# A bias table written two heads at a time in another stage, and Gram products of a recurrence taken in pairs

## The chip, the cores and the metric

One Trainium2 chip; the program uses one of its cores. The number compared is the device time of one execution in microseconds (us). The kernel before takes 2935.22 us, the median of three executions (2934.0 to 2938.29).

## The reference

Two blocks follow one another on 1024 tokens of width 1024, all in float32. The first has two layers. Layer 0 mixes by trailing means over 2, 4, 8 and 16 tokens, then a feed-forward part. Layer 1 is an attention over a window of 128 tokens, whose logits get a bias that depends on head and distance only:

```python
bias = rel_bias[t5_bucket(jnp.maximum(d, 0))]        # d = query - key, 16 heads
logits = logits + bias ...; logits = where(valid, logits, -inf)
```

Then again a feed-forward part. The second block projects the tokens and has two branches; one is a recurrence with eight heads of 64, in which every token updates a 64 x 64 state:

```python
sa = einsum('bhij,bhj->bhi', S, a_t)                  # a = -kk, b = kk * iclr ("ab" in the kernel)
S = S * w_t + sa[..., None] * b_t + v_t[..., None] * k_t
y = einsum('bhij,bhj->bhi', S, r_t)
```

## The kernel before, in words

The program is a row of stages. Each stage has one instruction list for each engine, and the next stage's lists start only when all engines have ended theirs, SyncE's (SP's) included. TensorE runs each float32 product as two matmul records.

**Pooling stage** (`pool_stage`, line 199). Nine tiles (16 meta tokens, then eight of 128). SP's list (line 240) loads x tiles six ahead, and at each tile t loads tile t + 6 if there is one (tiles 6 to 8 at t = 0 to 2) and stores tile t (`keep`, line 245), after the tile is made. It ends with a wait until all stores have landed.

**Projection stage of the attention** (`layer1_mixer`, line 1473, through `project_features`, line 881). Ten chunks of weights, numbered m = 0 to 9: keys, values, then eight of queries. A chunk is loaded (512 KB) by SP, multiplied by a gain on VectorE (line 988), split in a high and a low part on ScalarE (line 949) and VectorE (line 992), and multiplied on TensorE in two column slices of 24 matmuls each (lines 1032 to 1034). Three raw buffers. Three guests add work at each m:
- `KeyValueGuest` duplicates the keys by two DMAs at m = 4 (lines 1310, 1311) and turns the values at m = 4 to 6: three transposes on TensorE (line 1333), one copy on VectorE (line 1339). The transposes of m wait for the copy of m - 1.
- `BiasGuest` (line 1180): at m = 1 one matmul (line 1220) makes the bias by distance, 16 heads on 16 partitions x 384, which VectorE copies (line 1225). At m = 3 SP writes it to DRAM 128 times a head, one DMA of 3 MB (line 1203). At m = 7 it is read back with a shifted row for each partition (line 1208).
- `AdaGuest` (line 1228): eight loads of 1.5 MB (line 1254), for k = m - 1, each after the sum of k - 2, and one sum on VectorE each (line 1278).

In SP's list the load of chunk m stands after the guests of m - 1. In VectorE's list the order at m is: split of m + 1, gain of m + 2, the values' copy, the sum of k = m - 1.

**Recurrence** (`recurrence_stage`, line 1890). Eight tiles of 128 tokens, two chunks of 64 in each. The loop over tiles has ten half steps h. At each h TensorE works for three tiles at once: the preparation of tile t + 1, the inversion of tile t (lines 2261, 2273, 2275) and the chain through the state of tile t - 1. All products are of 64 x 64 by 64 columns, placed on one of four quarters of the array. Products of keys and reads are "Gram" products (line 2202): `inner` at h = 3 (24: ab with kk, eight of them twice, in the two orders of rows that are needed), `keys` at h = 6 (16: k with kk) and, in the chain, `rbk` at h = 4 (32: ab with r and k with r), 72 in a tile. VectorE masks them from the buffer `work_ps` (lines 2113, 2115, 2120, 2149). The tensors r and kk are planes 0 to 3 and 12 to 15 of one buffer, PB. At the start SP loads the masks, the bonus and the gates (1.5 MB) that only the stage after needs (line 2500).

Of the kernel before, what the change touches and what calls it, by code (L numbers as in the profile page):

```python
# [10 lines left out]
P = 128  # L11
# [187 lines left out]
def pool_stage(b, residual, store, post_gain, pre_gain):  # L199
# [6 lines left out]
    with b.stage() as ctx:  # L206
# [21 lines left out]
            "ss1", "sd1", "r1", "xg", "x", "ss2", "sd2", "r2", "xn", "tp", "xh", "xl", "stored")}  # L228

# [6 lines left out]
        with nc.Block() as block:  # L236
            @block.sync
            def _(sp):
# [22 lines left out]
                load(5)  # L261
                for t in range(N):
                    if t + XS < N:
                        load(t + XS)
                    keep(t)
                sp.wait_ge(s["stored"], 16 * N)

            @block.gpsimd
            def _(pool):
                pool.memset(b.eps[:, :], EPS).then_inc(s["eps"], 1)  # L270
                pool.wait_ge(s["bands"], 16)
# [49 lines left out]
            def _(dve):  # L321
# [6 lines left out]
                for k in range(N + 5):  # L328
# [34 lines left out]
                    if k + 2 < N:  # L363
                        inverted(k + 2)

            @block.tensor
            def _(pe):
# [7 lines left out]
                for k in range(N + 4):  # L375
                    if k < N:
# [15 lines left out]
                        if k == 0:  # L392
                            warm(3)
                    t = k - 4
                    if 0 <= t < N:
                        r = rows(t)
                        if t == 0:
                            pe.wait_ge(s["gains"], 48)
                        pe.wait_ge(s["xn"], t + 1)
# [780 lines left out]
class BiasGuest(Guest):  # L1180

    W = 3 * P

    def __init__(self, b, ctx, bias_rows, sinks):
        self.b, self.bias_rows, self.sinks = b, bias_rows, sinks
        self.table = b.nc.dram_tensor("bias_table", [HEADS, P, self.W], f32, kind="Internal").ap()
        self.rel = b.sb(ctx, "rel", [33, HEADS])
        self.hot = b.sb(ctx, "hot", [33, self.W])
        self.g = b.sb(ctx, "bias_by_offset", [HEADS, self.W])
        self.pb = b.ps(ctx, "pb", [HEADS, 512])  # L1190
        self.s_in, self.s_neg, self.s_g, self.s_ge, self.s_out, self.s_read = (
            b.sem(ctx, n) for n in ("bias_in", "bias_neg", "bias_g", "bias_ge", "bias_out", "bias_read"))

    def sync(self, sp, m):
        ins, table = self.b.ins, self.table
        if m == 0:
            sp.dma_start(self.rel[0:32, :], ins["rel_bias"]).then_inc(self.s_in, 16)
            sp.dma_start(self.hot[:, :], ins["cst"][0:33, C_HOT:C_HOT + self.W]).then_inc(self.s_in, 16)
            sp.dma_start(self.sinks[:, :], rows_of(ins["sinks"][0])).then_inc(self.s_in, 16)
# [4 lines left out]
        if m == 7:  # L1204
            sp.wait_ge(self.s_out, 16)

            skew = bass.AP(tensor=table.tensor, offset=P - 1, ap=[[self.W - 1, P], [P * self.W, HEADS], [1, 2 * P]])
            sp.dma_start(self.bias_rows[:, :, :], skew).then_inc(self.s_read, 16)
        if m > 7 and m == self.end:
            sp.wait_ge(self.s_read, 16)  # L1210
# [5 lines left out]
    def tensor(self, pe, m):  # L1216
        if m == 1:
            pe.wait_ge(self.s_in, 48)
            pe.wait_ge(self.s_neg, 1)
            pe.matmul(self.pb[:, 0:self.W], self.rel[:, :], self.hot[:, :], start=True, stop=True).then_inc(self.s_g, 1)  # L1220

    def vector(self, dve, m):
        if m == 1:
            dve.wait_ge(self.s_g, 1)
            dve.tensor_copy(self.g[:, :], self.pb[:, 0:self.W]).then_inc(self.s_ge, 1)
# [247 lines left out]
def layer1_mixer(b, residual_out, x1, ada_rows):  # L1473

    ins = b.ins
    with b.stage() as ctx:
# [6 lines left out]
        with b.stage() as c2:  # L1483
# [13 lines left out]
            bias = BiasGuest(b, c2, bias_rows, sinks)  # L1497
# [392 lines left out]
def recurrence_stage(b, PB, kk, ab, lw, tris, later):  # L1890
# [7 lines left out]
    with b.stage() as ctx:  # L1898
# [8 lines left out]
        RBK = b.sb(ctx, "RBK", [P, 2, DA])  # L1907
# [19 lines left out]
        pa = marks("pe_pre", ["cum", "ab", "ak", "tx", "tab", "tkv"])  # L1927
# [4 lines left out]
        pd = marks("pe_chain", ["ys0", "sa0", "st0", "rbk", "sa1", "ys1", "y0", "st1", "y1"])  # L1932
# [5 lines left out]
        da = marks("dve_pre", ["at", "bt", "kt", "lt", "xm", "rt", "ak"])  # L1938
        dl = marks("dve_add", [f"a{h}" for h in halves])
        dd = marks("dve_chain", ["sa00", "sa01", "sx0", "s0", "rb", "rk", "sa10", "sa11", "sx1", "s1"])  # L1940
# [34 lines left out]
        def natural():  # L1975
            quarters = wk[:, :, :].rearrange("p e (i x) -> p (e i) x", i=2)
            return quarters[:, 0:4:3].rearrange("p e (g x) -> p g e x", g=2)
# [7 lines left out]
        with nc.Block() as block:  # L1985
# [10 lines left out]
            def _(pool):  # L1996
# [3 lines left out]
                def other(t, l):  # L2000
                    da.wait(pool, t, "lt")
# [95 lines left out]
            def _(dve):  # L2097
# [12 lines left out]
                def masked(t):  # L2110
                    pa.wait(dve, t, "ab")
                    po.wait(dve, t - 2, f"u{LV - 1}")
                    da.mark(dve.tensor_tensor(LT[:, t % 2], natural(), wide(trix), ALU.mult), "lt")
                    pw.wait(dve, t - 2, "uu")
                    da.mark(dve.tensor_tensor(turned(t), wk[:, :, 0:4 * H].rearrange("p e (g x) -> p g e x", g=2), wide(lvl[0]), ALU.mult), "xm")

                def keys(t):
                    pa.wait(dve, t, "ak")
                    pm.wait(dve, t - 1, "mv")
                    da.mark(dve.tensor_tensor(halves_of(AK[:, :]), wk[:, :, 0:4 * H].rearrange("p e (g x) -> p e g x", g=2), wide(trix), ALU.mult), "ak")  # L2120
# [24 lines left out]
                def reads(t):  # L2145
                    pd.wait(dve, t, "rbk")
                    pd.wait(dve, t - 1, "y1")
                    for i, n in enumerate(("rb", "rk")):
                        dd.mark(dve.tensor_tensor(halves_of(RBK[:, i]), wk[:, :, 4 * H * i:4 * H * (i + 1)].rearrange("p e (g x) -> p e g x", g=2), wide(triu), ALU.mult), n)

# [3 lines left out]
                dve.wait_ge(s_in, 32)  # L2154
                masked(0)
                decayed(0, "rt")
                keys(0)
                for t in range(NT + 1):
                    more = t + 1 < NT
                    for h in halves:  # L2160
# [9 lines left out]
                        if h == 2 and more:  # L2170
                            decayed(t + 1, "kt")
                        if h == 3:
# [4 lines left out]
                        if h == 4 and t:  # L2177
                            stepped(t - 1, 0)
                            reads(t - 1)
                        if h == 5:  # L2180
                            if t:
                                applied(t - 1, 1)
                            if more:
                                decayed(t + 1, "rt")
# [6 lines left out]
            def _(pe):  # L2191
# [8 lines left out]
                def gram(left, right, t, e, c, q, place, part):  # L2200
                    o = 4 * H * part + H * c
                    return pe.matmul(wk[place, e, o:o + H], left[rows(e), c, chunk(t, q)], right[rows(e), c, chunk(t, q)], start=True, stop=True)

                def inner(t):
                    da.wait(pe, t, "bt")
# [4 lines left out]
                    for c in range(4):  # L2210
                        for q in range(2):
                            for e in range(2):
                                gram(ab, kk, t, e, c, q, at(e, q), 0)
                            mm = gram(ab, kk, t, 1, c, q, rows(q), 1)
                    pa.mark(mm, "ab")

                def keys(t):
                    da.wait(pe, t, "kt")
                    if t:
                        am.wait(pe, t - 1, "mv")  # L2220
                    else:
                        da.wait(pe, t, "xm")
                    for c in range(4):
                        for q in range(2):
                            for e in range(2):
                                mm = gram(k, kk, t, e, c, q, at(e, q), 0)
                    pa.mark(mm, "ak")

                def inverse_start(t):
                    pi.wait(pe, t, "eye")  # L2230
                    da.wait(pe, t, "ak")
# [46 lines left out]
                def values(t):  # L2278
                    da.wait(pe, t, "ak")
                    aa.wait(pe, t, "tkv")  # L2280
                    if t:
                        dd.wait(pe, t - 1, "rk")
                    else:
                        da.wait(pe, t + 1, "xm")
# [27 lines left out]
                def chain(t, n):  # L2312
# [27 lines left out]
                    elif n == "rbk":  # L2340
                        if t + 2 < NT:
                            da.wait(pe, t + 2, "xm")
                        else:
                            aw.wait(pe, t, "wt")
                        for c in range(4):
                            for i, left in enumerate((ab, k)):
                                for q in range(2):
                                    for e in range(2):
                                        mm = gram(left, r, t, e, c, q, at(e, q), i)
                    else:  # L2350
                        dd.wait(pe, t, "rk")
                        dd.wait(pe, t, "sx1" if q else "sa01")
                        for c in range(4):
                            for i, left in ((0, SA), (1, T[:, t % 3, 3])):
                                for e in range(2):
                                    mm = pe.matmul(yp[rows(e), P * c + H * q:P * c + H * (q + 1)], left[at(e, q), head(e, c)], RBK[at(e, q), i, head(e, c)],
# [4 lines left out]
                inner(0)  # L2361
                keys(0)
# [5 lines left out]
                steps = {1: ("ys0",), 3: ("sa0",), 4: ("st0", "rbk"), 5: ("sa1", "ys1"), 6: ("y0",), 7: ("st1",), 8: ("y1",)}  # L2368
                for t in range(NT + 1):
                    more = t + 1 < NT  # L2370
                    for h in halves:
# [7 lines left out]
                        if more:  # L2379
                            if h == 3:  # L2380
                                inner(t + 1)
# [312 lines left out]
```

## Time and profile before

| | |
|---|---|
| median of three executions | 2935.22 us |
| the profiled execution | 2935.99 us, of which span 2934.3 us |
| mean granted TensorE clock | 0.956 of full |
| pooling stage | 0 to 93 us |
| projection stage of the attention | 898 to 1061 us |
| recurrence | 2472 to 2748 us |

How to read it: the two long feed-forward stages (93 to 890 us and 1200 to 2000 us) keep TensorE busy nearly throughout; the change touches the other parts. PE is TensorE's matmul side, PEld its weight load, DVE VectorE, ACT ScalarE, POOL GpSimd, SPq SyncE's list. A wait row gives the engine and line that waited and what ended the wait; "issue" means that the profile shows nothing that it waited for. The share of DMA is of 16 engines.

### The profile page before, as it was taken

The page shows a single profiled execution, that of the slowest core. Times are in us where ns is not written, and L with a number is a line of the kernel's source. Part 1 is how long each engine was busy: PE and PEld are TensorE (multiplying, and loading weights), DVE is VectorE, ACT ScalarE, POOL GpSimd, SP SyncE. Part 2 cuts the span into 40 slices and gives each one's busy share as a digit, 9 for nine tenths or more (in the row PEclk, how much of TensorE's full clock was granted, in tenths as well). Part 3 has the DMA queues.
Part 4 walks back from the last instruction along what each step waited for, and adds up shares of the span by engine and source line. Part 5 has one row for each costly group of instructions (what it writes and reads, how often), then busy time and mean ns, then how long its engine had stood idle before and what let it go on. Part 6 is the DMA issues. An engine that isn't in the chain of part 4 may idle for free. (4 is left out here: it accounts for less than half of the span.)

```text
span 2934.3 us, 48957 instructions
## 1 busy us (share of the span) xinstructions
PE 2673.6 (91%) x20693; PEld 2221.3 (76%) x20693; DVE 1240.5 (42%) x2037; ACT 782.1 (27%) x1479; POOL 286.5 (10%) x190
## 2 busy tenths in 40 slices
PE   9799999999997699879999999999789998777776
PEld 8799999999986566667888888887577776766455
DVE  6333333333343458362333333333424553544447
ACT  6311111111153159342211111112221412233221
POOL 2100000000021025120000000002300000222102
PEclk9899999999998799989999999999899998999878
DMA  4211111111035500222111111112312112000032
GB/s 145 79 44 51 55 45 43 43 43 43 29 121 125 193 25 2 94 101 86 44 64 43 43 43 43 43 50 93 108 35 83 44 65 95 4 4 4 3 122 101
DMA packets 63099, 183.66 MB, mean 63 GB/s; under 512 B 10469, under 2 KB 19846, under 8 KB 61518
## 3 DMA queue, kind: packets, MB, share of 16 engines
q1 hardware_dynamic: 62928, 181.18, 18.6%
q8 instruction: 132, 2.16, 0.3%
q14 instruction: 39, 0.32, 0.0%
HBM read 150.54 MB, written 30.03 MB: 62 GB/s over the span
## 5 line engine op out<-in xcount | busy, mean ns | idle before, releaser
L790 PE MATMUL f0gu<-b1XH,f0w0H 128*128 128x346 f32 (+1 forms) x528 | 170.2, 322 | 6.9 <-DVE f0w0L L722 6.3
L742 DVE TENSOR_TENSOR f1hf<-f1sg,f1gu 128x512 f32<-128x512 f32 x44 | 30.3, 688 | 337.7 <-ACT f1sg L689 337.7
L742 DVE TENSOR_TENSOR f0hf<-f0sg,f0gu 128x346 f32<-128x346 f32 (+1 forms) x66 | 34.1, 516 | 326.2 <-ACT f0sg L689 326.2
L753 DVE TENSOR_TENSOR Y<-f0dn,Y 128x512 f32<-128x512 f32 (+1 forms) x180 | 124.0, 689 | 113.6 <-PE f0dn L837 112.7
L792 PE MATMUL f0gu<-b1XH,f0w0L 128*128 128x346 f32 (+1 forms) x528 | 170.3, 322 | 0.0
L791 PE MATMUL f0gu<-b1XL,f0w0H 128*128 128x346 f32 (+1 forms) x528 | 169.7, 321 | 0.0
L792 PE MATMUL f0gu<-b1XH,f0w1L 128*128 128x346 f32 (+1 forms) x528 | 169.7, 321 | 0.0
L790 PE MATMUL f0gu<-b1XH,f0w1H 128*128 128x346 f32 (+1 forms) x528 | 169.3, 321 | 0.0
L791 PE MATMUL f0gu<-b1XL,f0w1H 128*128 128x346 f32 (+1 forms) x528 | 169.0, 320 | 0.0
L753 DVE TENSOR_TENSOR Y<-f1dn,Y 128x512 f32<-128x512 f32 x160 | 109.2, 690 | 90.7 <-PE f1dn L837 90.7
L790 PE MATMUL f1gu<-b1XH,f1w0H 128*128 128x512 f32 x352 | 139.5, 396 | 6.3 <-DVE f1w0L L722 6.3
L835 PE MATMUL f0dn<-f0dH,f0hH 128*128 128x512 f32 (+1 forms) x360 | 142.5, 396 | 0.0
L836 PE MATMUL f0dn<-f0dL,f0hH 128*128 128x512 f32 (+1 forms) x360 | 142.3, 395 | 0.0
L837 PE MATMUL f0dn<-f0dH,f0hL 128*128 128x512 f32 (+1 forms) x360 | 140.9, 391 | 0.0
L791 PE MATMUL f1gu<-b1XL,f1w0H 128*128 128x512 f32 x352 | 140.0, 398 | 0.0
L792 PE MATMUL f1gu<-b1XH,f1w0L 128*128 128x512 f32 x352 | 139.3, 396 | 0.0
L791 PE MATMUL f1gu<-b1XL,f1w1H 128*128 128x512 f32 x352 | 139.2, 395 | 0.0
L790 PE MATMUL f1gu<-b1XH,f1w1H 128*128 128x512 f32 x352 | 138.2, 393 | 0.8 <-DVE f1hf L742 0.8
L792 PE MATMUL f1gu<-b1XH,f1w1L 128*128 128x512 f32 x352 | 138.4, 393 | 0.0
L689 ACT ACTIVATE f0sg<-f0gu 128x346 f32<-128x346 f32 (+1 forms) x66 | 30.4, 461 | 365.0 <-PE f0gu L792 365.0
L835 PE MATMUL f1dn<-f1dH,f1hH 128*128 128x512 f32 x320 | 126.9, 397 | 0.0
L836 PE MATMUL f1dn<-f1dL,f1hH 128*128 128x512 f32 x320 | 126.8, 396 | 0.0
(402 smaller groups left out, 6587.5 us busy)
## 6 DMA issues: line engine op xcount, KB each, us to landing
f0raw<-in_w_gate_up SPq DMA_DIRECT2D x43, 512.0 KB, 5.7
f1raw<-in_w_gate_up SPq DMA_DIRECT2D x43, 512.0 KB, 5.6
residual<-Y SPq DMA_DIRECT2D x32, 512.0 KB, 2.8
Y<-in_w_ada SPq DMA_DIRECT2D x8, 1536.0 KB, 6.8
f0rawd<-in_w_down SPq DMA_DIRECT2D x22, 512.0 KB, 3.3
f1rawd<-in_w_down SPq DMA_DIRECT2D x22, 512.0 KB, 3.3
w_in_b_raw<-in_w_in_b SPq DMA_DIRECT2D x16, 512.0 KB, 3.4
w_in_a_raw<-in_w_in SPq DMA_DIRECT2D x11, 512.0 KB, 4.3
```

The lines of the kernel that those rows point to most:

```text
L689: act.activation(sg[:, i, 0:w], gu[:, i, 0, 0:w], ACT.Silu).then_inc(s["silu"], 1)
L742: dve.tensor_tensor(hf[:, i, 0:w], sg[:, i, 0:w], gu[:, i, 1, 0:w], ALU.mult).then_inc(s["mul"], 1)
L753: dve.tensor_tensor(y, dn[0:r, (par * ND + i) % 4], y, ALU.add).then_inc(s["acc"], 1)
L790: pe.matmul(o, wH[c][:, j, k], xh, start=(k == 0), stop=False)
L791: pe.matmul(o, wH[c][:, j, k], xl, start=False, stop=False)
L792: last = pe.matmul(o, wL[c][:, j, k], xh, start=False, stop=(k == KC - 1))
L835: pe.matmul(o, hh, wh, start=(n == 0), stop=False)
L836: pe.matmul(o, hh, wl, start=False, stop=False)
L837: last = pe.matmul(o, hl, wh, start=False, stop=(n == len(parts) - 1))
```

## The change

The bias by distance is made in the pooling stage: its inputs are loaded after the first x tiles, the matmul and the copy come at step 1. At each of the tiles t = 0 to 7 SP writes two heads of the table (393 KB) behind the tile's store, and SP's list ends with a wait until all eight have landed. The guest of the projection stage only reads, four heads at each m from 5 to 8.

In the recurrence a product takes ab (or k) with the pair r and kk at once, 128 columns. `inner` has 16 such products, `keys` 16, the eight products in the other order of rows are a step of their own (`inner_odd`, at h = 4, after the mask "rb"). `rbk` and its masks leave the chain; the masks "rb" and "rk" are made with the preparation into a buffer for three tiles. The decay of r moves from h = 5 to h = 2. The load of the gates moves to the stage after.

```diff
+    def sync_table(self, sp, t):
+        if t < HEADS // self.PART:
+            if t == 0:
+                sp.wait_ge(self.s_ge, 1)
+            heads = slice(self.PART * t, self.PART * (t + 1))
+            copies = self.g[heads, :].rearrange("h (o w) -> h o w", o=1).broadcast_to([self.PART, P, self.W])
+            sp.dma_start(self.table[heads], copies).then_inc(self.s_out, 16)
...
                 for t in range(N):
                     if t + XS < N:
                         load(t + XS)
                     keep(t)
+                    bias.sync_table(sp, t)
                 sp.wait_ge(s["stored"], 16 * N)
+                bias.sync_end(sp)
...
-        if m == 3:
-            sp.wait_ge(self.s_ge, 1)
-            sp.dma_start(table, self.g[:, :].rearrange("h (o w) -> h o w", o=1).broadcast_to([HEADS, P, self.W])).then_inc(self.s_out, 16)
...
+        if 5 <= m < 5 + HEADS // self.PART:
+            sp.dma_start(self.bias_rows[:, h:h + self.PART, :], skew).then_inc(self.s_read, 16)
...
+                def both(left, t, e, c, q):
+                    pair = PB[rows(e), c:c + 13:12, chunk(t, q)]
+                    return pe.matmul(wk[at(e, q), e, 2 * H * c:2 * H * (c + 1)], left[rows(e), c, chunk(t, q)], pair, start=True, stop=True)
...
                 def inner(t):
-                    da.wait(pe, t, "bt")
+                    da.wait(pe, t, "rt")
...
+                def inner_odd(t):
+                    da.wait(pe, t, "rb")
...
                 def keys(t):
-                    da.wait(pe, t, "kt")
+                    da.wait(pe, t, "lt1")
...
-                steps = {1: ("ys0",), 3: ("sa0",), 4: ("st0", "rbk"), 5: ("sa1", "ys1"), 6: ("y0",), 7: ("st1",), 8: ("y1",)}
+                steps = {1: ("ys0",), 3: ("sa0",), 4: ("st0",), 5: ("sa1", "ys1"), 6: ("y0",), 7: ("st1",), 8: ("y1",)}
```

## Rows read from the trace of the kernel before

**Rows 1.** the page, part 1: busy us (share of the span), instructions.

```profile
PE 2673.6 (91%) x20693; PEld 2221.3 (76%) x20693; DVE 1240.5 (42%) x2037; ACT 782.1 (27%) x1479; POOL 286.5 (10%) x190
```

**Rows 2.** waits of PE, 890 to 1075 us: total us, times, longest us.

```profile
PE w_q_pr L1032 <- DVE w_q_wL L992: 17.3, 1, 17.3
...
PE turned_values L1333 <- DVE V L1339: 6.5, 1, 6.5
```

**Rows 3.** windows: us, busy PE PEld DVE ACT POOL, PEclk, DMA share, GB/s.

```profile
974.60:988.70 14.10, 14.10 (x48) 10.92 (x48) 5.69 (x3) 1.65 (x2) 0.00 (x0) 0.79 0.50 189
...
995.20:1009.40 14.20, 14.20 (x52) 11.38 (x53) 7.50 (x5) 1.28 (x2) 0.00 (x0) 0.79 0.70 252
1009.60:1043.20 33.60, 33.60 (x147) 26.98 (x145) 18.06 (x10) 7.09 (x9) 0.00 (x0) 1.00 0.39 142
```

**Rows 4.** DMA issues, 895 to 1010 us: KB each, us to landing.

```profile
w_q_raw<-in_w_q SPq DMA_DIRECT2D x6, 512.0 KB, 7.7
bias_table<-bias_by_offset SPq DMA_DIRECT2D x1, 3072.0 KB, 34.3
```

**Rows 5.** timeline of SP in it: start us, us that the issue took.

```profile
926.51 0.69 SPq L1203 DMA_DIRECT2D bias_table<-bias_by_offset  x1
929.84 7.43 SPq L1254 DMA_DIRECT2D Y<-in_w_ada  x1
```

**Rows 6.** DMA, 928 to 960 us: packets, MB, share of 16 engines.

```profile
q1 hardware_dynamic: 2027, 3.12, 92.3%
...
w_q_raw<-in_w_q SPq DMA_DIRECT2D x1, 512.0 KB, 31.5
```

**Rows 7.** timeline of PE at 919.6 us.

```profile
919.62 0.82 PE L1220 MATMUL pb<-hot,rel 33*16 33x384 f32 x2
```

**Rows 8.** timeline of DVE in the projection stage.

```profile
982.04 3.41 DVE L1278 SCALAR_TENSOR_TENSOR Y<-Y,cs 128x3072 f32<-128x3072 f32 x1
...
995.03 3.41 DVE L1278 SCALAR_TENSOR_TENSOR Y<-Y,cs 128x3072 f32<-128x3072 f32 x1
```

**Rows 9.** DMA, 1049 to 1051 us: one transfer, from one partition.

```profile
q1 hardware_dynamic: 2, 0.01, 1.5%
```

**Rows 10.** DMA, 2749 to 2757 us: five transfers, one of their issues.

```profile
q1 hardware_dynamic: 592, 0.10, 7.7%
...
gn_back<-in_cst SPq DMA_DIRECT2D x1, 16.0 KB
```

**Rows 11.** timeline of SP in the pooling stage and at the next stage's start.

```profile
27.12 0.43 SPq L247 DMA_DIRECT2D residual<-Y  x1
...
40.02 41.45 SPq L247 DMA_DIRECT2D residual<-Y  x7
93.25 1.76 SPq L628 DMA_DIRECT2D f0raw<-in_w_gate_up  x4
```

**Rows 12.** DMA packets of one load and one store, 34 to 39.9 us.

```profile
q1 hardware_dynamic: 288, 1.05, 55.6%
```

**Rows 13.** timeline of DVE at the pooling stage's end.

```profile
91.24 1.22 DVE L332 TENSOR_TENSOR b1XL<-pool_tp,b1XH 128x1024 fp32r<-128x1024 f32 x1 [3.18 <-ACT b1XH L316]
```

**Rows 14.** waits of PE, five tiles: first and last of ten on issue.

```profile
PE inv_ps L2275 <- issue: 9.5, 8, 1.4
...
PE work_ps L2288 <- issue: 0.8, 1, 0.8
```

**Rows 15.** one window between two such waits.

```profile
2598.06:2602.18 4.12, 2.60 (x127) 1.00 0.03 6
```

**Rows 16.** DMA of the same five tiles, 2535 to 2694 us.

```profile
q8 instruction: 40, 0.66, 1.8%
```

**Rows 17.** timeline of DVE in one tile of the recurrence.

```profile
2591.85 1.29 DVE L2149 TENSOR_TENSOR RBK<-work_ps,masks 128x512 f32<-128x512 f32 x2 [0.90 <-PE work_ps L2202]
```

**Rows 18.** tile gates_in: ns min/median/max, first to last start; then its load.

```profile
L2500 DVE TENSOR_TENSOR PB<-gates_in,PB x6: 677/900/1781, 2783.1 to 2791.6; 128x512 f32<-128x512 f32 x6
...
DMA to landing us min/median/max: 12.5/12.5/12.5
```

More of the change, by code:

```diff
@@ L196, in linker, with pool_stage @@
     return link
-def pool_stage(b, residual, store, post_gain, pre_gain):
+def pool_stage(b, residual, store, post_gain, pre_gain, bias):
     nc, ins = b.nc, b.ins
@@ L261, in _ @@
                 load(5)
+                bias.sync_inputs(sp)
                 for t in range(N):
@@ L270, in _ @@
                 pool.memset(b.eps[:, :], EPS).then_inc(s["eps"], 1)
+                pool.wait_ge(s["eps"], 1)
+                bias.gpsimd(pool)
                 pool.wait_ge(s["bands"], 16)
@@ L364, in _ @@
                         inverted(k + 2)
+                    if k == 1:
+                        bias.vector(dve)
             @block.tensor
@@ L393, in _ @@
                             warm(3)
+                        if k == 1:
+                            bias.tensor(pe)
                     t = k - 4
@@ L398, in _ @@
                             pe.wait_ge(s["gains"], 48)
+                            bias.emptied(pe)
                         pe.wait_ge(s["xn"], t + 1)
@@ L1214, in gpsimd, with tensor, vector, emptied @@
         pool.wait_ge(self.s_neg, 1)
[L1216 to L1225, printed above, removed]
+    def tensor(self, pe):
+        pe.wait_ge(self.s_in, 32)
+        pe.wait_ge(self.s_neg, 1)
+        pe.matmul(self.pb, self.rel[:, :], self.hot[:, :], start=True, stop=True).then_inc(self.s_g, 1)
+    def vector(self, dve):
+        dve.wait_ge(self.s_g, 1)
+        dve.tensor_copy(self.g[:, :], self.pb).then_inc(self.s_ge, 1)
+    def emptied(self, pe):
+        pe.wait_ge(self.s_ge, 1)
+class BiasGuest(Guest):
+    PART = 4
+    def __init__(self, b, ctx, table, bias_rows, sinks):
+        self.b, self.table, self.bias_rows, self.sinks = b, table, bias_rows, sinks
+        self.s_in, self.s_read = (b.sem(ctx, n) for n in ("sinks_in", "bias_read"))
+    def sync(self, sp, m):
+        W = BiasTable.W
+        if m == 0:
+            sp.dma_start(self.sinks[:, :], rows_of(self.b.ins["sinks"][0])).then_inc(self.s_in, 16)
+        if 5 <= m < 5 + HEADS // self.PART:
+            h = self.PART * (m - 5)
+            skew = bass.AP(tensor=self.table.tensor, offset=P * W * h + P - 1, ap=[[W - 1, P], [P * W, self.PART], [1, 2 * P]])
+            sp.dma_start(self.bias_rows[:, h:h + self.PART, :], skew).then_inc(self.s_read, 16)
+        if m == self.end:
+            sp.wait_ge(self.s_read, 16 * (HEADS // self.PART))
+            sp.wait_ge(self.s_in, 16)
 class AdaGuest(Guest):
@@ L1496, in layer1_mixer @@
             kvg = KeyValueGuest(b, c2, KT, VT, V)
-            bias = BiasGuest(b, c2, bias_rows, sinks)
+            bias = BiasGuest(b, c2, bias_table.table, bias_rows, sinks)
             bias.end = len(chunks)
@@ L2000, in other @@
                 def other(t, l):
-                    da.wait(pool, t, "lt")
+                    da.wait(pool, t, "lt1")
                     if l >= 3:
@@ L2176, in _ @@
                                 masked(t + 1)
[L2177 to L2180, printed above, removed]
+                        if h == 4:
                             if t:
-                                applied(t - 1, 1)
+                                stepped(t - 1, 0)
                             if more:
-                                decayed(t + 1, "rt")
+                                odd(t + 1)
+                        if h == 5 and t:
+                            applied(t - 1, 1)
                         if h == 6 and more:
@@ L2212, in inner @@
                             for e in range(2):
-                                gram(ab, kk, t, e, c, q, at(e, q), 0)
-                            mm = gram(ab, kk, t, 1, c, q, rows(q), 1)
+                                mm = both(ab, t, e, c, q)
                     pa.mark(mm, "ab")
+                def inner_odd(t):
+                    da.wait(pe, t, "rb")
+                    for c in range(4):
+                        for q in range(2):
+                            mm = pe.matmul(wk[rows(q), 1, H * c:H * (c + 1)], ab[rows(1), c, chunk(t, q)], kk[rows(1), c, chunk(t, q)], start=True, stop=True)
+                    pa.mark(mm, "ab1")
                 def keys(t):
-                    da.wait(pe, t, "kt")
                     if t:
                         am.wait(pe, t - 1, "mv")
-                    else:
-                        da.wait(pe, t, "xm")
+                    da.wait(pe, t, "lt1")
                     for c in range(4):
@@ L2280, in values @@
                     aa.wait(pe, t, "tkv")
[L2281 to L2284, printed above, removed]
+                    da.wait(pe, min(t + 1, NT - 1), "lt1")
+                    if t == NT - 1:
+                        aw.wait(pe, t - 1, "wt")
                     for c in range(4):
@@ L2339, in chain @@
                                     mm = pe.matmul(ch[rows(e), H * c:H * (c + 1)], T[at(e, q), t % 3, i, head(e, c)], right[at(e, q), head(e, c)], start=(i == 2), stop=(i == 1))
[L2340 to L2349, printed above, removed]
                     else:
-                        dd.wait(pe, t, "rk")
+                        da.wait(pe, t, "rk")
                         dd.wait(pe, t, "sx1" if q else "sa01")
@@ L2361, in _ @@
                 inner(0)
+                inner_odd(0)
                 keys(0)
@@ L2381, in _ @@
                                 inner(t + 1)
+                            if h == 4:
+                                inner_odd(t + 1)
                             if h == 6:
@@ L2398, in _, with recurrent_output @@
                             update(t - 1, HL - 1)
-def recurrent_output(b, PB, bv, gates):
+def recurrent_output(b, PB, bv, later, gates):
     nc, ins = b.nc, b.ins
@@ L2413, in recurrent_output @@
         pp = b.ps(ctx, "gn_ps", [P, 4, 512])
-        s = {n: b.sem(ctx, "gn_" + n) for n in ("in", "eps", "mm", "dve", "act", "sq", "rs", "aff", "sum", "out")}
+        s = {n: b.sem(ctx, "gn_" + n) for n in ("in", "eps", "mm", "dve", "act", "sq", "rs", "aff", "sum", "out", "gates")}
         units = [("mean", i) for i in range(8)] + [("var", i) for i in range(2)] + [("back", i) for i in range(8)]
@@ L2435, in _ @@
                 sp.dma_start(cols[:, 1], ins["gn_b_2"]).then_inc(s["in"], 16)
+                sp.dma_start(*later).then_inc(s["gates"], 16)
             @block.gpsimd
```

106 lines of the change are left out of this document (58 added, 48 removed).

## The prediction

> **What bounds the kernel now.** I read the page first: TensorE has a matmul in flight for 2673.6 us of the 2934.3 [rows 1]. So a change pays only where TensorE idles or loses instructions, and hurts where it makes a stage end later. The waits of TensorE by stage come next. In the projection stage two waits stand out, 17.3 and 6.5 us, each once [rows 2]. The windows behind them show what follows an idle stretch: the granted clock is 0.79 on average, part of the chunk at the lower level (1.2 GHz), and it takes 14.1 and 14.2 us, where three later chunks at full clock take 33.6 together, 11.2 each [rows 3]. Third, the recurrence: in five tiles (2535 to 2694 us) ten kinds of wait end in "issue", together 35.1 us, the largest 9.5, the smallest 0.8 [rows 14]: 7.0 us a tile of 31.8. Last, the pooling stage, where I look at SP's list and at the last work [rows 11, 13].
>
> **Part 1, the table leaves the projection stage.** The table's DMA takes 34.3 us to land [rows 4]. Behind it in SP's list stands the load of w_ada, whose issue alone takes 7.43 us [rows 5]; the chunk load after it lands 31.5 us after its issue [rows 6], where 7.7 us is the median [rows 4]. That is the wait of 17.3 us: a chunk whose weights come late. With the table gone I walk the loop again. It has its own period: load of the next chunk 7.7, gain and copy about 1.8, sum 3.4, together 13.0 us, as the sums stand apart [rows 8]. TensorE needs 11.2 a chunk, so the loop is the slower one, but it runs ahead. The sum of m = 1 ends at 929, that of m = 8 then at about 1011. TensorE starts the fourth chunk after the keys at 957 without a wait and wants the last sum at 957 + 5 x 11.2 = 1013. It fits, by 2 us. The copies of the values (wait of 6.5) come earlier in the same way. The sum of what leaves: 17.3 + 6.5 [rows 2], the slow clock 14.1 - 11.2 = 2.9 and 14.2 - 11.2 - 0.3 for the transposes = 2.7 [rows 3], and the bias matmul 0.8 [rows 7]. Together 30.2 us. The four reads at m = 5 to 8 stand behind the chunk loads and hide. Bounds: if the loop slips by a microsecond a turn, TensorE waits again for some 6, so 24; not over 32.
>
> **Part 2, the table enters the pooling stage.** Two heads are two partitions, and the question is how many DMA engines such a transfer gets. The trace shows it by the small packets at the end of each transfer. A transfer from one partition has 2 packets: its data and one end [rows 9]. Five transfers with 128, 128, 8, 128 and 128 partitions have 592 [rows 10]: 4 x (128 + 16) + 8 + 8. So 8 partitions end 8 times, on 8 engines, not on 16, and I take 2 engines for 2 partitions. Each then carries 128 packets of 1536 B for every transfer, 1024 in all, one after another.
>
> What is one packet worth? Before, 16 engines at once held 2027 packets in 32 us: each starts one every 16 x 32 / 2027 = 0.253 us and is busy 92.3% of it [rows 6]. That is 98 GB/s together, 6 a partition. It is no limit of a partition: the single transfer moves 12 KB in 1.5% of 16 x 2 us = 0.48 us, 26 GB/s [rows 9]. Something is shared, then. The lower bound for a lone stream is 1536 B at 26 GB/s = 0.06 plus the unoccupied 0.02 = 0.08 us; the upper 0.253. I take half of 0.253, 0.125 us: four neighbouring partitions got 24.5 GB/s together, nearly the 26 of one stream, so two streams from neighbours should share about that.
>
> So the eight transfers hold two engines for 1024 x 0.125 = 128 us. On the same two engines lie shares of the later x loads (tiles 7 and 8) and of eight stores, ten transfers; one load and one store took 55.6% of 5.9 us [rows 12], 1.64 each, so 16.4 us. The first table issue stands behind the store at 27.1 [rows 11], packets flow at about 29. The engines are never free in between, since SP issues a table every 7 us (seven stores in 41.45 us) and each takes 16. End: 29 + 128 + 16.4 = 173.4, and 0.8 for the hand-over (the last work before ends at 92.46 [rows 13], the next stage's first issue is at 93.25 [rows 11]). The pooling stage is then 174.2 - 93.25 = 80.9 us longer. The wait at the end of SP's list carries it: nothing of the feed-forward stage may start before. Stalls inside the stage (the load of tile 8 lands perhaps 25 us late and TensorE, VectorE and ScalarE wait for it) cost nothing more, as the table ends later anyway. The matmul and the copy at step 1 are under 2 us beneath it. Bounds: 0.08 a packet gives +35, 0.253 gives +212.
>
> The Trainium skill speaks against this change in "DMA: Bandwidth & Descriptors", section "Why a DMA increments its semaphore by 16 and not by 1": a transfer runs on the largest k up to 16 that divides the slowest dimension of both sides, so k = 2 here. By that rule too the sum is +80.9; without it, with 16 engines, it would be about +1. The trace agrees, with its 592 packets.
>
> **Part 3, the recurrence.** 72 Gram products in a tile become 40, with the same columns: 32 x 128 + 8 x 64 = 72 x 64. So the matmuls' streaming hardly changes, but 32 x 4 = 128 instructions go (two matmul and two load records each). What is that worth? The waits on "issue" come every 127 matmul records, as in the window of 4.12 us with 2.60 busy [rows 15], and in 159 us the instruction queue moves 40 packets, 0.66 MB, 16 KB each [rows 16]: 3.98 us a packet. 128 instructions are half a packet. If the packet sets the pace, a tile gains 2.0 us; if only its idle time goes, 0.5 x 35.1 / 36 (the ten rows count 36 times) = 0.5; if the chain between engines takes over, 0. I take 1.2: the masks of rbk, 1.29 us on VectorE between rbk and what follows [rows 17], leave the chain, but the new wait of `inner_odd` for "rb" stands in TensorE's list before product and update of h = 4, and the masks of h = 3 are 0.4 us longer. Behind it the inversion of tile t waits. Eight tiles: -9.6. The start pays: before the first inversion now stand the decay of r, the masks rb and rk (0.65 each by half of 1.29 [rows 17]), the extra step with its own mask (about 1), and longer key products at the low clock: +3.9. Net -5.7, bounds -12 and +4. The gates' load takes 12.5 us and is first needed at 2783 [rows 18], 30 us after its new issue: nothing.
>
> The skill's "Runtime: NRT & Kernel Launch", section "Instruction fetch mechanics", calls the 16 KB block's cost mostly hidden. The rows disagree: 0.98 us idle at each. By the page the part would be worth 0 a tile and the sum 9.6 higher.
>
> **Sum.** 2935.99 (profiled execution) + 80.9 - 30.2 - 5.7 = 2981.0; that execution is 0.8 above the median, so 2980.
>
> **Rivals.** (A) The writes spread over all 16 engines. Place: the pooling stage; price 34.3 / 8 = 4.3 us a transfer between tiles 7 us apart, beside 3.3 of load and store, so at most +1. Time 2936 + 1 - 30.2 - 5.7 = 2901. For it: the old transfer did spread. Against: it had 16 partitions, and 8 gave 8. This is the side "faster"; the sign turns where the writes cost less than 35.9 us of stage, at 0.08 us a packet. (B) Two engines, but each as slow as before: 0.253 a packet, 3112. For it: it is the only measured rate of this packet. Against: 16 streams then, 2 now. (C) Two engines at the lone stream's rate, 0.08: 2935, no change. Against: the neighbours' 24.5 GB/s. (D) The DMA issue that blocks SP (7.43 us) acts in the pooling stage: it delays tiles, but ends inside the 80.9.
>
> **How the numbers follow.** Forecast (0.10 to 0.16 us a packet, 2955 to 3020) 0.63; A 0.12; B and all above 0.16, 0.12; C, below 0.10, 0.13. The range leaves out most of A and the far part of B: 2925 to 3045. A measurement of this kernel tells 0.2% (6 us) from no change. Faster 0.16 (A and a third of C), same 0.06, slower 0.78.
>
> **What would show it.** Right: SP's first issue of the next stage near 174 us; packets of 1536 B with two end packets a transfer, and a DMA share near 2/16 from 90 to 170 us; no wait of TensorE over 3 us between the chunks of the projection stage, and that stage 30 us shorter; instruction packets down from about 8.2 to 7.7 a tile, tiles 1.2 us shorter. Wrong: a pooling stage that ends at 94 us (A), or at 300 (B); the wait of 17.3 us still there with no table before it.

## The result and the profile after

The changed kernel takes 2979.34 us (median of four executions, 2969.07 to 2984.37), the kernel before beside it 2936.76 (2934.0 to 2946.13). The ratio is 1.0138, interval 1.0118 to 1.0158: 42.6 us slower, where 2980, or +44, was forecast.

The profiled execution is the fastest of the four (2969.07 us, span 2967.4), 33.1 over the span before. By the first start of each stage's work in both traces:

| stage | before, us | after, us | difference | forecast |
|---|---|---|---|---|
| pooling | 93.2 | 173.4 | +80.2 | +80.9 |
| projection | 163.8 | 132.5 | -31.3 | -30.2 |
| recurrence | 277.2 | 266.3 | -10.9 | -5.7 |
| all else | 2400.1 | 2395.2 | -4.9 | 0 |

No edit reaches the last row but for the gates' load. 3.2 of it is the output stage, whose length also differs between executions of kernels that have the same one. The median is 10 us above this execution; in which stage those lie, one trace can't say. The four executions lie within 15 us.

The page after, part 1, against [rows 1]: 512 matmul records fewer (64 in each of 8 tiles), 9.9 us less busy.

```profile
PE 2663.7 (90%) x20181; PEld 2215.5 (75%) x20181; DVE 1240.0 (42%) x2053; ACT 781.5 (26%) x1479; POOL 285.4 (10%) x190
```

**Pooling stage.** SP's list after (start us, us that the issue took), against [rows 11]. The table issues (L1219) begin at 31.21. Once two table transfers have not landed, issues take long: the load behind the second table issue takes 11.99 us, and the next store behind each later one 13 to 16. In the kernel before none of this stage took over half a microsecond from 26 us on. The last row is the next stage's first load: 173.43.

```profile
31.21 0.78 SPq L1219 DMA_DIRECT2D bias_table<-bias_by_offset  x1
...
43.24 11.99 SPq L244 DMA_DIRECT2D xin<-in_x  x1
...
59.21 13.42 SPq L248 DMA_DIRECT2D residual<-Y  x1
72.67 1.96 SPq L1219 DMA_DIRECT2D bias_table<-bias_by_offset  x1
74.67 15.68 SPq L248 DMA_DIRECT2D residual<-Y  x1
...
141.91 3.07 SPq L1219 DMA_DIRECT2D bias_table<-bias_by_offset  x1
145.03 14.29 SPq L248 DMA_DIRECT2D residual<-Y  x1
173.43 1.77 SPq L639 DMA_DIRECT2D f0raw<-in_w_gate_up  x4
```

DMA of the kernel after, 90 to 170 us. "GB/s" is in 40 slices of 2 us: between the stores it stands at 23 to 26. The engines' share is 19.1%, 3 of 16, with the five stores in it; the last row is a window with nothing but table packets (112 to 117 us), and there it is 11.4%, 1.8 of 16. Two streams of 1536 B packets at 25 GB/s together are 0.123 us a packet.

```profile
GB/s 235 43 25 24 26 24 46 23 62 201 24 23 23 23 38 44 23 142 121 23 23 23 22 45 46 25 240 25 25 26 25 41 44 25 57 208 24 24 25 34
...
q1 hardware_dynamic: 1900, 4.40, 19.1%
...
q1 hardware_dynamic: 74, 0.11, 11.4%
```

TensorE pays for it in one piece: its longest wait before 180 us is for the next stage's first weights.

```profile
PE f0gu L801 <- DVE f0w0L L733: 73.5, 1, 73.5
```

**Projection stage.** The view of TensorE's waits from 979 to 1112 us has one row left, at the start, where the weights come first. The 17.3 and the 6.5 of [rows 2] are gone, and the granted clock of the stage is 0.97.

```profile
PE w_q_pr L1043 <- DVE w_q_wL L993: 8.6, 1, 8.6
...
979.50:1112.00 132.50, 125.58 (x549) 0.97 0.43 156
```

The four reads of the table hide between the chunk loads, which land in 7.3 us (KB each, us to landing), not 7.7 with one of 31.5 [rows 4, 6].

```profile
w_q_raw<-in_w_q SPq DMA_DIRECT2D x8, 512.0 KB, 7.3
bias_rows<-bias_table SPq DMA_DIRECT2D x4, 512.0 KB, 8.1
```

**Recurrence.** The state S is written 16 times, twice a tile. The rows give the first and last start, before and then after: 218.7 us and 202.7 between them, so 16.0 less. The first stands 55.6 us behind the stage's start before and 60.6 after: the beginning is 5.0 longer. Nine more traces below have the same recurrence with the joint product: there the two times are 203.4 to 207.2 us and 59.2 to 61.0, and the stage takes 265.9 to 269.9. So this trace is at the low end, and the difference of 16.0 is 11.5 to 16.0 over all of them.

```profile
L2143 DVE TENSOR_TENSOR S<-Sx,ein x16: 424/424/428, 2528.1 to 2746.8; 128x256 f32<-128x256 f32 x16
```

```profile
L2199 DVE TENSOR_TENSOR S<-Sx,ein x16: 424/424/426, 2581.8 to 2784.5; 128x256 f32<-128x256 f32 x16
```

The instruction queue moved 67 packets in the whole stage before (2472.5 to 2749.7 us) and 63 after (2521.2 to 2787.5), four fewer:

```profile
q8 instruction: 67, 1.10, 1.7%
...
q8 instruction: 63, 1.03, 1.7%
```

### The profile page after: what moved, and what is told of

It reads as the page before. It is cut to its first block and busy times, and to the rows that moved or that the text cites. A ratio compares the mean times of both kernels' runs of the same rounds, so it can differ in the third digit from the quotient of the medians.

```text
span 2967.4 us, 47959 instructions
## 1 busy us (share of the span) xinstructions
PE 2663.7 (90%) x20181; PEld 2215.5 (75%) x20181; DVE 1240.0 (42%) x2053; ACT 781.5 (26%) x1479; POOL 285.4 (10%) x190
## 5 line engine op out<-in xcount | busy, mean ns | idle before, releaser
L753 DVE TENSOR_TENSOR f1hf<-f1sg,f1gu 128x512 f32<-128x512 f32 x44 | 30.2, 687 | 337.9 <-ACT f1sg L700 337.9
L801 PEld LDWEIGHTS f0gu<-b1XH,f0w0H 128*128 128x128 f32 x528 | 100.2, 190 | 75.2 <-DVE f0w0L L733 73.9
```

Source lines behind the costliest of these rows:

```text
L753: dve.tensor_tensor(hf[:, i, 0:w], sg[:, i, 0:w], gu[:, i, 1, 0:w], ALU.mult).then_inc(s["mul"], 1)
L801: pe.matmul(o, wH[c][:, j, k], xh, start=(k == 0), stop=False)
```

## The experiments

The number behind a label is the median; the ratio to the kernel before, timed beside it, has a 95% interval. First the change taken apart.

**The table alone**: 2982.11 us, ratio 1.0168 (1.0144 to 1.0191). Pooling and projection stages as after the change, the whole recurrence (and the gates' load) as before:

```diff
-                def both(left, t, e, c, q):
-                    pair = PB[rows(e), c:c + 13:12, chunk(t, q)]
...
-                steps = {1: ("ys0",), 3: ("sa0",), 4: ("st0",), 5: ("sa1", "ys1"), 6: ("y0",), 7: ("st1",), 8: ("y1",)}
+                steps = {1: ("ys0",), 3: ("sa0",), 4: ("st0", "rbk"), 5: ("sa1", "ys1"), 6: ("y0",), 7: ("st1",), 8: ("y1",)}
```

> The kernel before with the table alone moved (pooling stage writes it two heads a tile, the projection stage only reads it); recurrence and gates as before. Theory (two engines carry the table, the parts add): pooling stage ends near 174 us instead of 93 (+80), projection stage 31 shorter, nothing else: 2936 + 80 - 31 = 2985 us. Rival (the parts interact, part of the stage gain comes from the recurrence edit): the projection stage is shorter by clearly less than 31.

Pooling ended at 174.0 and the projection took 134.5, so the theory holds (2985 forecast).

**The recurrence alone**: 2922.76 us, ratio 0.9963 (0.9949 to 0.9977). The recurrence as after, the table made and written in the projection stage as before:

```diff
-                    bias.sync_table(sp, t)
...
+        if m == 3:
+            sp.wait_ge(self.s_ge, 1)
+            sp.dma_start(table, self.g[:, :].rearrange("h (o w) -> h o w", o=1).broadcast_to([HEADS, P, self.W])).then_inc(self.s_out, 16)
```

> The kernel before with the recurrence, its output stage and the place of the gates' load as in the changed kernel; the table as before. Theory of the prediction (1.2 us a tile, start dearer by 4): 2930 us. What the trace after suggests: recurrence 277 -> 266 us and the output stage 44 -> 41, so 2922 us. Rival (the traces' difference is chance of one execution): 2936, same.

The time is the one that the trace suggested (2922), not the prediction's 2930. The recurrence took 266.5, and the old waits of the projection are all there, so it is the table that removes them:

```profile
PE w_q_pr L1032 <- DVE w_q_wL L992: 17.2, 1, 17.2
...
PE turned_values L1333 <- DVE V L1339: 7.5, 1, 7.5
```

The two halves, +49.4 and -10.0 against the 2932.75 of their comparison, add to +39.4; the whole, timed beside another execution of the kernel before, gave +42.6. Each of these has an interval of 4 to 7 us to either side, and within it they don't interact.

**The same bytes, other partitions.** Five kernels move the same 3.1 MB in the same packets of 1536 B and differ in which heads a transfer takes, that is, in its source partitions. The rows of the table in DRAM that it writes differ with them; no run moves one without the other. First, every transfer takes all 16 heads, 16 rows of each:

```diff
-            heads = slice(self.PART * t, self.PART * (t + 1))
-            copies = self.g[heads, :].rearrange("h (o w) -> h o w", o=1).broadcast_to([self.PART, P, self.W])
-            sp.dma_start(self.table[heads], copies).then_inc(self.s_out, 16)
+            rows = slice(HEADS * t, HEADS * (t + 1))
+            copies = self.g[:, :].rearrange("h (o w) -> h o w", o=1).broadcast_to([HEADS, HEADS, self.W])
+            sp.dma_start(self.table[:, rows], copies).then_inc(self.s_out, 16)
```

> The changed kernel, but each of the eight DMAs writes 16 of the 128 copies of all 16 heads (outer dimension 16 on both sides) in place of 128 copies of two heads: same bytes, same number of issues, same place. Theory (two engines were the whole cost): each transfer takes some 4 us on 16 engines, the pooling stage ends at 93 to 96 us, time 2890 to 2900 us, faster than both kernels. Rival (packets of 1536 B from SBUF or the wait at the stage's end cost it whatever the spread): the pooling stage stays over 120 us long.

2900.13 us, ratio 0.9886 (0.9869 to 0.9902); the next stage starts at 101.4, the projection takes 134.4. That is rival A's time, and it beats both kernels. The stage ends 5 us later than the 93 to 96 that was expected; the last group of experiments takes that up.

Two heads a transfer, but eight partitions apart:

```diff
-            heads = slice(self.PART * t, self.PART * (t + 1))
+            heads = slice(t, t + 9, 8)
```

> The changed kernel, but the two heads of a tile are t and t + 8 in place of 2t and 2t + 1, so the two source partitions are eight apart; still two engines, same packets. Theory (neighbouring partitions share a path of about 25 GB/s, a lone stream gets about 0.08 us a packet): transfers of 10 us, the pooling stage ends near 128 us, time about 2934. Rival (0.125 us is what one engine needs for such a packet, whatever its neighbour does): stage and time as in the changed kernel, 173 and 2979 us.

2920.08 us, ratio 0.9949 (0.9932 to 0.9966); pooling ended at 119.7. The rival (2979) falls. The theory has the direction but not the size (2934 forecast): between the stores the rate is 51 GB/s, twice that of two neighbours, with two engines as before, which is 0.06 us a packet and not 0.08. In the last slices, after the store, it is 22 to 27, the rate of one stream: the reading is that one engine ends before the other (95 to 118 us, 0.6 us a slice):

```profile
GB/s 48 54 30 28 25 37 51 51 48 321 393 212 50 47 43 51 51 48 53 48 43 28 28 26 51 51 48 51 309 402 198 26 25 24 27 24 27 24 22 21
```

Four heads a transfer, four transfers: neighbours, then four apart (the second line in place of the first):

```diff
-    PART = 2
+    PART = 4
...
             heads = slice(self.PART * t, self.PART * (t + 1))
+            heads = slice(t, t + 13, 4)
```

> Kernel after with four neighbouring heads a transfer (heads 4t to 4t+3, from four neighbouring partitions), in four transfers beside the pooling stage's tiles 0 to 3 instead of two heads in each of eight. All else as in the changed kernel. Theory (neighbouring partitions share one path of about 25 GB/s, whatever number of DMA engines reads them): four engines at 0.25 us a packet, 4 x 128 x 0.25 = 128 us as before; the pooling stage ends at about 170 to 176, total about 2979. Rival (each DMA engine has 0.125 us a packet of its own): four engines at 0.125, 64 us in all, table ready by about 100, pooling ends at about 105 to 115, total about 2915.

> The same four transfers of four heads, but of heads t, t+4, t+8, t+12, so that no two source partitions are neighbours or in one group of four. Theory (the shared path is that of neighbouring partitions): each of four engines at 0.065 to 0.07 us a packet as in the heads-apart kernel, 4 x 128 x 0.07 = 36 us in all, hidden beside the stage's tiles; the pooling stage ends at 98 to 104, total about 2897 to 2903, as with the table spread over all sixteen partitions. Rival (number of engines alone counts, and partitions do not): as the four-neighbours kernel of this same set, whatever that gives.

Four neighbours: 2958.66 us, ratio 1.0098 (1.0067 to 1.0128), pooling to 157.4. Four apart: 2901.02, ratio 0.9886 (0.9868 to 0.9903), to 97.5. DMA of both: neighbours 45 to 75 us, where they again get 23 to 25 GB/s between loads and stores, and apart 60 to 70 us, where they get about 100:

```profile
GB/s 25 117 307 170 23 23 216 336 46 25 25 20 25 23 23 46 25 25 25 25 20 25 23 23 25 25 25 44 61 44 80 101 107 95 48 24 25 25 25 27
```

```profile
GB/s 98 98 98 104 119 86 80 86 98 104 98 104 98 113 98 100 131 82 100 115 86 104 98 98 98 98 104 360 383 410 377 410 400 399 393 410 377 328 170 98
```

So the number of engines is not what limits. The rival "0.125 us for each engine" said 2915 for the neighbours and falls. They came out 20 us under my 2979 though: there are stretches in which the table alone moves at more than 25 GB/s. The rows below count packets of four neighbours from 52 to 64 us and from 94 to 100: 184 table packets in 12 us are 23.6 GB/s, and 187 in 6 us (those under 2 KB less those under 512 B) are 47.9.

```profile
DMA packets 185, 0.30 MB, mean 25 GB/s; under 512 B 0, under 2 KB 184, under 8 KB 184
```

```profile
DMA packets 216, 0.39 MB, mean 64 GB/s; under 512 B 5, under 2 KB 192, under 8 KB 216
```

The four engines don't end a transfer together. In this trace their last writes of the second transfer land at 91.3, 96.1, 99.4 and 100.2 us, so from 91.3 on one is already in the next four heads while others are still in the old ones, and the doubled rate falls in that stretch. Two groups at work give twice the rate of one, as with two heads apart.

All sixteen heads in one transfer behind the last input load:

```diff
-        if t < HEADS // self.PART:
+        if t == 2:
...
+            sp.dma_start(self.table, self.g[:, :].rearrange("h (o w) -> h o w", o=1).broadcast_to([HEADS, P, self.W])).then_inc(self.s_out, 16)
```

> The spread table written by one transfer of all sixteen heads, issued behind the pooling stage's last input load (tile 2), instead of eight transfers of 16 partitions x 16 rows. Theory (sixteen partitions on sixteen engines give about 98 GB/s in either form; 3.1 MB are then 32 us from about 50 us on, done by about 85 to 90): hidden, total 2897 to 2902, as with eight. Rival (one long transfer holds the residual stores behind it on each engine's queue, and so the stage's end): the pooling stage ends at 105 to 125, total 2903 to 2925.

2899.71 us, ratio 0.9881 (0.9859 to 0.9902); the stage ends at 98.4. Sixteen partitions: 92 to 98 GB/s with 88.4% of all engines' time (55 to 65 us), no more than four partitions apart had with four engines. This is as the theory said; the rival (105 to 125) falls.

**The recurrence.** The joint product split in two of 64 columns, otherwise the spread table:

```diff
-                    return pe.matmul(wk[at(e, q), e, 2 * H * c:2 * H * (c + 1)], left[rows(e), c, chunk(t, q)], pair, start=True, stop=True)
+                    for i, right in enumerate((r, kk)):
+                        mm = pe.matmul(wk[at(e, q), e, H * (2 * c + i):H * (2 * c + i + 1)], left[rows(e), c, chunk(t, q)], right[rows(e), c, chunk(t, q)], start=True, stop=True)
+                    return mm
```

> The spread-table kernel (2900.1), with the recurrence's joint product of 128 columns issued as two products of 64 columns each (operand order, waits and columns as after the change): 32 matmuls more a tile, 8 tiles, nothing else. Theory (the change's gain in the recurrence is the fewer TensorE instructions, through their fetching, about 1 us idle for every 127 matmul records, and their fixed cost, not the other order of waits): the recurrence is again 274 to 278 us, 8 to 11 more than with the joint product; total about 2909 to 2911. Rival (the gain is that the two separate waits of the second product are gone): the recurrence stays at 266, total within 2 us of 2900.

2911.74 us, ratio 0.992 (0.9903 to 0.9938), so 11 to 14 us over kernels with the joint product (2898.2 to 2901.0); in the trace the recurrence took 281.7, 15.8 more than in the first trace of the spread table, 12.4 more than in the second. That is even above my 274 to 278, and it is the 277.2 of before plus the 5.0 of the longer beginning. The rival (gain from the waits that went) falls: with the new waits and the old instructions nothing is gained.

The opposite: the instructions kept, columns taken away.

```diff
-                    return pe.matmul(wk[at(e, q), e, 2 * H * c:2 * H * (c + 1)], left[rows(e), c, chunk(t, q)], pair, start=True, stop=True)
+                    return pe.matmul(wk[at(e, q), e, 2 * H * c + H:2 * H * (c + 1)], left[rows(e), c, chunk(t, q)], kk[rows(e), c, chunk(t, q)], start=True, stop=True)
```

> The spread-table kernel, with the joint product of the recurrence computing only its 64 columns for kk and leaving out the 64 for r (the instructions, their number, order and waits are as before; the output is not the reference's). It takes away 32 x 2 x 64 columns a tile, 1.7 us a tile at 2.4 GHz. Theory (in the steady recurrence TensorE is paced by its instructions, a block of 127 matmul records each 3.7 to 3.9 us, and a block's idle time shrinks or grows with what its columns leave): the recurrence stays at 264 to 267, total 2897 to 2902. Rival (TensorE is bound by columns, and the fetching adds a fixed 1 us a block): the recurrence is 12 to 14 us shorter, about 253, total about 2887.

2899.93 us, ratio 0.9872 (0.9848 to 0.9896), beside 2898.23 for the spread table. The recurrence took 266.3, where the joint product took 265.9 to 269.9: 1.7 us of columns less in each tile, some 14 in all, bring nothing that shows. Windows of 204 us in the steady part (us, PE busy with its matmul records, PEclk, DMA share, GB/s), of before, after, split product and fewer columns:

```profile
2510.00:2714.00 204.00, 152.69 (x6658) 1.00 0.02 4
```

```profile
2559.00:2763.00 204.00, 162.18 (x6659) 1.00 0.02 4
```

```profile
2489.00:2693.00 204.00, 153.85 (x6630) 1.00 0.02 4
```

```profile
2489.00:2693.00 204.00, 156.94 (x6627) 1.00 0.02 4
```

The busy time differs by 9.5 us, the number of records by 32 in some 6650; the spread table, the base of the last two, has 163.58 us and 6695 records in its own window. So the records per microsecond agree within 1%, the busy times do not. What gives way is the idle time: TensorE's waits on "issue" in these windows sum to 44.5 us before and 34.4 after. The instruction queue (packets, MB, share), after and with fewer columns, in the same windows; before has 53 packets too:

```profile
q8 instruction: 53, 0.87, 1.8%
```

```profile
q8 instruction: 53, 0.87, 1.7%
```

204 / 53 = 3.85 us for each packet of 16 KB, and 6659 / 53 = 126 matmul records in it. The packet sets the pace; longer products only fill its time.

**The start of the pooling stage.** With the table hidden, the stage still ends 3 to 8 us later than before. It is late from its start: the first store is issued at 27.1 us before, at 35.3 with the spread table and at 32.1 with one transfer. Three kernels and the spread table again:

> The spread-table kernel unchanged, once more, as the base for the three kernels beside it (their differences are under one per cent). Expected by every theory: 2897 to 2903, ratio to before 0.988 to 0.990; recurrence 266, pooling stage until 98 to 102.

The spread table again: 2898.23 us, ratio 0.9861 (0.9839 to 0.9883), stage to 101.5. The matmul and the copy at step 3:

```diff
-                        if k == 1:
+                        if k == 3:
                             bias.tensor(pe)
...
-                    if k == 1:
+                    if k == 3:
                         bias.vector(dve)
```

> The spread-table kernel with the bias table's one matmul, and its copy out of PSUM, at step 3 of the pooling stage's loop instead of step 1. Theory (at step 1 TensorE waits for the one-hot rows, which land behind the stage's own loads, and its clock then falls: the mixing matmuls of the first tiles run at 1.2 GHz for 4 to 5 us, and the stage is 4 to 8 us late): the pooling stage ends at 93 to 97 instead of 98 to 102, total 2892 to 2897. Rival (the lateness is from the extra loads on the DMA queues, not from TensorE's wait): nothing changes, 2897 to 2903.

2897.14 us, ratio 0.9855 (0.9832 to 0.9878), stage to 99.8: not told from the base, as the rival said, though that doesn't show that the extra loads are the cause. The theory said that the wait at step 1 costs the clock. But without it the clock fell here too. Windows of 5 us (us, PE busy, PEclk), late sum, and then late sum with one transfer, whose lists are the same up to there:

```profile
20.00:25.00 5.00, 5.00 (x19) 0.55 0.00 1
25.00:30.00 5.00, 5.00 (x37) 0.77 0.01 3
```

```profile
20.00:25.00 5.00, 5.00 (x36) 1.00 0.00 0
25.00:30.00 5.00, 5.00 (x47) 1.00 0.02 3
```

The clock differs although the lists are the same up to there (the spread table, traced twice, had 0.54 and 0.55 from 20 to 25 us); what decides it stays open. It isn't the whole of the lateness either: the second of these executions has the full clock, and its stage still ends 3.4 us later than before.

> Both at once: one transfer of sixteen heads behind the last input load, and the bias table's matmul at step 3. Expected from the single ones: as the late bias sum (2892 to 2897) or 1 to 2 us better, since SP has only one issue to make between the stage's stores; if the one transfer then starts later and the stage's last stores queue behind it, 2 to 5 us worse than the late bias sum alone.

2896.02 us, ratio 0.9855 (0.9833 to 0.9877), stage to 96.7: the lowest median, 41 us under the kernel before, though not told apart from the three kernels beside it.

## Why the prediction was right

- **Part 2, +80.9, measured +80.2.** Two engines, 0.125 us a packet (measured 0.123 in the quiet slices), engines never free, the next stage at 174.2 (measured 173.4): each stood in the trace. The reason given, neighbours sharing one path of about 25 GB/s, was a guess from two rows [rows 6, 9] and is now borne out by runs: two neighbours 25 GB/s, two apart 51, four neighbours 25, four apart about 100, all sixteen 98. That the path is on the side of the partitions, and not of the DRAM rows that go with them, is the likely reading but isn't shown. Stalls inside the stage were there (the load of tile 8 took 25.6 us to land) and were covered, as predicted. Two smaller errors cancelled: no table packet started before 33.1 us, where 29 was forecast, and the packets and shares behind it took about 5 us less than the 144.4 forecast.
- **Rival A** had the right time for another kernel: with the writes on all engines the change brings 2896 to 2900, where it said 2901. **B** (0.253) and **C** (0.08) fall with the rate of 0.123. C's price was itself too high: two streams that don't share take 0.06 a packet. **D** was in the trace, 12 to 16 us an issue, and ended inside the 80.2.
- **The rule on engines** (the Trainium skill, "DMA: Bandwidth & Descriptors", section "Why a DMA increments its semaphore by 16 and not by 1") is borne out by the shares: two heads held 11.4% of the engines' time, 1.8 of 16, and sixteen heads 88.4%. The price of the packet was the larger question: with two engines, and other partitions, 54 of the 80 us go.
- **Part 1, -30.2, measured -31.3** (29.3 and 29.4 in the table-alone and the spread kernel). Both waits and the slow clock after them went, and no new wait came. The slack of 2 us that the walk gave the last sum held: the sum ends at 1091.15 us, and TensorE's first matmul that needs it starts at 1093.35.
- **Part 3, -5.7, measured -10.9.** The term that failed is "I take 1.2": it should have been nearer the 2.0 that stood beside it, "if the packet sets the pace". Eight tiles gave 16.0 in this trace and 11.5 to 15.3 in the others, not 9.6, and four instruction packets fewer at 3.85 us are 15.4. I went below since I gave weight to the order of waits (`inner_odd`, the masks); the split product shows that it costs nothing in the steady part (217.0 us from first S to last, 218.7 before). The beginning was +5.0 (3.6 to 5.4 in the others), predicted +3.9. The two errors were opposite, and 5.2 us net in this trace. By the page of the Trainium skill that calls the block's cost mostly hidden ("Runtime: NRT & Kernel Launch", section "Instruction fetch mechanics") the part had been worth nothing; the 16.0 us measured here decide against it.
- **The sum.** In the traces it is +33.1 against +45.1 forecast: part 3 gave 5.2 more, and 4.9 came from stages that no part of the prediction touched. The medians differ by 42.6. The mechanisms hold, but that the median fits the forecast within 1 us, closer than the terms do, is luck.

## What to carry to other kernels

- Before a small DMA is spread over idle moments, count the source partitions of each transfer and look which ones they are. The bytes and the packets of data were the same in all of these kernels; the choice of heads for a transfer made 80 us of stage, or 3 to 8. Slice along the axis that keeps all partitions in every transfer.
- Where waits on "issue" come at even counts of instructions, compare records per microsecond in two windows with different busy time. If they agree, count instructions, not columns: fewer, longer products pay at up to the full price of the packet.
- A stage's end that waits for its DMAs turns a hidden transfer into the stage's length at once; the sum for a moved transfer is start + packets per engine x time of a packet, checked against what else lies on that engine.

## What the runs showed of the hardware

- DMA writes from four neighbouring SBUF partitions (tested with 0 to 3, 4 to 7 and so on, packets of 1536 B) to as many neighbouring stretches of DRAM got 25 GB/s together, whether two or four engines moved them. Two such groups gave 51, four about 100. That the groups are these four and not others is read from 2, 4 and 16 partitions only, and that it is the partitions and not the DRAM side isn't shown.
- While a stream holds its engines, SP's issue of another DMA takes up to 15.7 us behind two engines and 26.6 us behind four neighbours. Behind one large transfer on sixteen engines it took at most 6.1 us, and behind the eight spread ones at most 3.4.
- A straight list of small matmuls ran at one 16 KB instruction packet each 3.85 us, some 126 matmul records, at full clock and with 75 to 80% of the time busy.
